# Differential attention: GpSimd scales and adds the two exponentials from the thirteenth step on

## The chip, the cores and the metric

One core of one Trainium2 chip. The time is device microseconds of one execution; three runs of the kernel before are given. Engines: TensorE (PE in the profile, its weight loads PEld), VectorE (DVE), ScalarE (ACT), GpSimd (POOL), SyncE (SP).

## What is computed

The program is two residual blocks of a model of width 1024 on 1024 rows, all in float32: an mLSTM and pooling mixer, a windowed attention, then a block with gated linear attention beside differential attention, a convolutional feed-forward part and a gated embedding. The change lies in the differential attention of the second block. Cut to what matters:

```python
for blk in range(T // Q_BLOCK):                       # 8 blocks of 128 queries
    q0 = blk * Q_BLOCK
    k_end = q0 + Q_BLOCK
    s = jnp.einsum('bqhmd,bkhmd->bhmqk', q[:, q0:k_end], k[:, :k_end])   # 4 heads, m = 0, 1
    s = jnp.where(mask, s, -1e30)
    pr = jax.nn.softmax(s, axis=-1)
    w = pr[:, :, 0] - lam * pr[:, :, 1]
    outs.append(jnp.einsum('bhqk,bkhd->bqhd', w, v[:, :k_end]))
o = rms_norm(jnp.concatenate(outs, axis=1), norm_g) * (1.0 - lam_init)
```

So for each block and head there are two softmaxes over the same keys, and the second is subtracted from the first with a factor before the product with the values.

## The kernel before

The parts of the second block are written as five instruction streams, one for each engine, that meet at semaphores; nothing reorders them. `diff_part` is one of these parts. Its work is 32 steps j = 4 bi + h (query block bi, head h), of width kw = 128 n columns, n = bi + 1 key chunks. What a step does, with the line in the profile:

- TensorE, `scores` (L3359): the products of queries and keys for m = 0 and 1 into the PSUM tile S. For j from 2 to 15 S holds two steps side by side (`s_at`), so that scores(j) wait for the maxima of step j-2; from step 16 it holds one, and scores(j) wait for both maxima of step j-1.
- VectorE, `biggest` (L3475), twice: reads S and the tile `chunk_mask`, writes the scaled, masked scores into `pb` (in the room of HT, so the profile calls it HT) and their maximum into `neg_max`. `pb` has four places, by j % 4.
- ScalarE, `probs` (L3417), twice: the exponential in place in `pb`, and its sum into `sums`.
- VectorE, `weights` (L3482, L3483, L3485): the reciprocal of the sums; the factor `second_share` (cw), one number for each row; and the combination, second exponential times factor plus first, into the first half of `pb`. Division by the first sum is left to the end of a block.
- TensorE, `turn` (L3369): n transposes of the combined tile into TP. ScalarE, `take` (L3425): TP to SBUF. TensorE, `pv` (L3378): the product with the values into O.
- Once a block: ScalarE's `norm` (L3431 and the root behind it), VectorE's `out` (L3491, L3493), TensorE's `turn_diff` (L3318), ScalarE's `diff_hi` (L3442) and VectorE's `diff_lo` (L3506), which split the result into a rounded high part and a low part for the next product.

The order on TensorE in loop index j is scores(j), turn(j-2), pv(j-3), on VectorE biggest(j, 0), biggest(j, 1), weights(j-1), on ScalarE probs(j, 0), take(j-2), probs(j, 1). In the loop indices 16 to 23 VectorE also does an eighth of a weight split each (L412). GpSimd's stream in this part loads the vectors for lambda, fills the mask (L3338, L3340) and loads a norm vector; the next thing in its queue is the load of rows for the output projection (L526), which waits for the last `diff_lo`.

Of the kernel before, what the change touches and what calls it, by code (L numbers as in the profile page):

```python
# [29 lines left out]
ALU = mybir.AluOpType  # L30
# [6 lines left out]
P = 128  # L37
# [3232 lines left out]
def diff_part(K, st, mix):  # L3270
# [7 lines left out]
    nc, i = K.nc, K.i  # L3278
    lam_init = 0.8 - 0.6 * math.exp(-0.3 * 0)
    NJ = 4 * XT  # L3280
    gla_steps = [1, 3, 5, 7, 9, 11, 13, 15]
    K.ZLr = [nc.alloc_sbuf_tensor_at("z_lo_gla", [P, XT, 4, P], F32R, offset=K.offset["Zg"]),
             nc.alloc_sbuf_tensor_at("z_lo_diff", [P, 4, T], F32R, offset=K.offset["dQT"])]
# [3 lines left out]
    pb = room[:, 0:8 * T].rearrange("p (j m n) -> p j m n", m=2, n=T)  # L3287
    wt = room[:, 8 * T:10 * T].rearrange("p (j n) -> p j n", n=T)
    nm = K.sb(st, "neg_max", [P, NJ, 2])
    sm = K.sb(st, "sums", [P, NJ, 2])  # L3290
    rc = K.sb(st, "recip_sums", [P, NJ, 2])
    cw = K.sb(st, "second_share", [P, NJ])
    lam = K.sb(st, "lam", [P, 4])
# [11 lines left out]
    s_in, s_nm, s_p, s_msk = K.sem("df_in"), K.sem("df_max"), K.sem("df_probs"), K.sem("df_mask")  # L3305
    s_s = [K.sem(f"df_scores{m}") for m in range(2)]
    s_w, s_t, s_tr, s_pv = K.sem("df_weights"), K.sem("df_turned"), K.sem("df_turned_read"), K.sem("df_pv")
    s_lam, s_le, s_rs, s_z = K.sem("df_lam_arg"), K.sem("df_lam_exp"), K.sem("df_rs"), K.sem("df_z")
    s_gt, s_gh, s_gl = K.sem("df_gla_turned"), K.sem("df_gla_hi"), K.sem("df_gla_lo")
    s_zt, s_zh, s_zl = K.sem("df_z_turned"), K.sem("df_z_hi"), K.sem("df_z_lo")  # L3310
# [19 lines left out]
    def s_at(j):  # L3330
        return 512 * ((j + 1) % 2) if 2 <= j < 16 else 0

    def gpsimd(g):
        mix.sines(g)
        for n, name in enumerate(("lam_q1_2", "lam_k1_2", "lam_q2_2", "lam_k2_2")):
            g.dma_start(lv[:, n, :], i[name].to_broadcast([P, 64])).then_inc(s_in, 16)
        mix.done(g)
        g.memset(msk[:, :], 0.0).then_inc(s_msk, 1)  # L3338
        g.wait_ge(s_msk, 1)
        g.memset(msk[0:64, T - 64:T], NEG).then_inc(s_msk, 1)  # L3340
        g.wait_ge(s_in, 64)
        g.dma_start(gn[:, :], i["diff_norm_2"].to_broadcast([P, 512])).then_inc(s_in, 16)

    def tensor(pe):
        def scores(j):
# [43 lines left out]

        for j in range(NJ + 6):  # L3390
            if j == 18:
                pe.wait_ge(s_gl, XT)
            if j < NJ and j % 4 == 0:
                mix.ready(pe, j // 4 + 1)
# [70 lines left out]
    def vector(v):  # L3465
        ch = Chain(v, K.v_chain, K.vn)
        mix.left(v)
        v.wait_ge(s_msk, 2)

        def biggest(j, m):  # L3470
            kw = (j // 4 + 1) * P
            v.wait_ge(s_s[m], j + 1)
            if j >= 4:
                v.wait_ge(s_t, j - 3)
            v.tensor_tensor_reduce(pb[:, j % 4, m, 0:kw], S[:, m, s_at(j):s_at(j) + kw], msk[:, T - kw:T], -0.125, -NEG,  # L3475
                                   ALU.add, ALU.min, nm[:, j, m:m + 1]).then_inc(s_nm, 1)

        def weights(j):

            kw = (j // 4 + 1) * P  # L3480
            v.wait_ge(s_p, 2 * j + 2)
            ch.link(v.reciprocal(rc[:, j, :], sm[:, j, :]))  # L3482
            ch.link(v.scalar_tensor_tensor(out=cw[:, j:j + 1], in0=sm[:, j, 0:1], scalar=lam[:, 3:4], in1=rc[:, j, 1:2],  # L3483
                                           op0=ALU.mult, op1=ALU.mult))
            v.scalar_tensor_tensor(out=pb[:, j % 4, 0, 0:kw], in0=pb[:, j % 4, 1, 0:kw], scalar=cw[:, j:j + 1],  # L3485
                                   in1=pb[:, j % 4, 0, 0:kw], op0=ALU.mult, op1=ALU.add).then_inc(s_w, 1)

        def out(bi):
            v.wait_ge(s_rs, bi + 1)
            r = ss[:, 1, bi, :]  # L3490
            ch.link(v.tensor_tensor(r, r, rc[:, 4 * bi:4 * bi + 4, 0], ALU.mult))  # L3491
            for h in range(4):
                ins = v.scalar_tensor_tensor(out=K.QT[:, h, bi * P:(bi + 1) * P], in0=O[:, bi % 2, h * P:(h + 1) * P],  # L3493
                                             scalar=ss[:, 1, bi, h:h + 1], in1=gn[:, h * P:(h + 1) * P],
                                             op0=ALU.mult, op1=ALU.mult)
            ins.then_inc(s_z, 1)

        def gla_lo(r):
            v.wait_ge(s_gh, r + 1)
            v.tensor_tensor(ZL[:, r, :, :], TP[:, 512:1024].rearrange("p (k t) -> p k t", t=P),  # L3500
                            K.ZH[:, 0:4, r * P:(r + 1) * P].bitcast(F32), ALU.subtract).then_inc(s_gl, 1)

        def diff_lo(bi):
            v.wait_ge(s_zh, bi + 1)
            at = slice(bi * P, (bi + 1) * P)
            v.tensor_tensor(ZLD[:, :, at], O[:, bi % 2, :].rearrange("p (k t) -> p k t", t=P),  # L3506
                            K.ZH[:, 4:8, at].bitcast(F32), ALU.subtract).then_inc(s_zl, 1)

        for j in range(NJ + 6):
            if 16 <= j < 24:  # L3510
                K.split_lo(v, ("out2", 0, 1), j - 16, 8)
            if j < NJ:
                biggest(j, 0)
                biggest(j, 1)
            if j == 0:
                v.wait_ge(s_in, 64)
                for n in range(2):
                    v.wait_ge(s_lam, n)
                    v.tensor_tensor_reduce(lp[:, :], lv[:, 2 * n, :], lv[:, 2 * n + 1, :], 1.0, 0.0, ALU.mult, ALU.add,
                                           lam[:, n:n + 1]).then_inc(s_lam, 1)  # L3520
            if j == 6:
                v.wait_ge(s_in, 80)
                ch(v.tensor_scalar(gn[:, :], gn[:, :], 1.0 - lam_init, None, ALU.mult))
            if j == 1:
                v.wait_ge(s_le, 1)

                ch.link(v.tensor_tensor(lam[:, 2:3], lam[:, 1:2], lam[:, 0:1], ALU.subtract))
                ch.link(v.tensor_scalar(lam[:, 3:4], lam[:, 2:3], -lam_init, None, ALU.add))
            if 1 <= j <= NJ:
                weights(j - 1)  # L3530
            if j - 1 in gla_steps:
                gla_lo((j - 1) // 2)
            if j >= 8 and j % 4 == 0:
                out((j - 8) // 4)
            if j >= 10 and j % 4 == 2:
                diff_lo((j - 10) // 4)
        diff_lo(XT - 1)
        K.vn = ch.n

    return Part(sync, gpsimd, tensor, scalar, vector, turn_diff, (XT - 1,), None, done, taken, done)  # L3540


# [470 lines left out]
def phase_gla_in(K):  # L4013
# [7 lines left out]
    with ExitStack() as st:  # L4021
        diff = diff_part(K, st, mix)
# [94 lines left out]
```

## Time and profile before

| | us |
|---|---|
| median of 3 runs | 3333.32 (3331.22 to 3338.41) |
| span of the profiled execution | 3330.9 |
| TensorE busy in it | 3262.9 (98%) |
| VectorE, ScalarE, GpSimd busy | 1781.2, 1524.0, 113.7 |

The page gives a span for the profiled execution and no other time; the span runs from the first to the last instruction. The stage of the change lies from about 2235 us (first scores) to 2357 us (first product of the output projection). Idle time of an engine counts where TensorE waits for it.

### The profile page before, as it was taken

Reading aid. Unit: us, or ns where it says so; the run is one execution under the profiler, and the core shown is the slowest. Engines: PE = TensorE matmul, PEld = TensorE weight load, DVE = VectorE, ACT = ScalarE, POOL = GpSimd, SP = SyncE. Lnnn points to the kernel's source line nnn. Section 1 sums busy time; section 2 is a strip of 40 time slices with the busy share of each in tenths; the row PEclk is TensorE's granted clock in tenths of the full one; section 3 lists DMA queues with packets and bytes.
Section 4 is the critical chain, followed back from the end, with each engine's and each line's share of the span. In section 5 each row is a group of like instructions: output and inputs, shape, how many; then the busy total and the mean of one; then the engine's idle time right before and its main releaser. Section 6 shows DMA issues by size and latency. Waiting matters only on the chain. (4 is left out here: it accounts for less than half of the span.)

```text
span 3330.9 us, 42983 instructions
## 1 busy us (share of the span) xinstructions
PE 3262.9 (98%) x17616; PEld 2669.0 (80%) x17616; DVE 1781.2 (53%) x2768; ACT 1524.0 (46%) x2424; POOL 113.7 (3%) x245
## 2 busy tenths in 40 slices
PE   7999999999999999999999999998999999999998
PEld 5988888898888787887887877776778888878886
DVE  7554444544445567532886634358556445444555
ACT  5343434434334345125786534228435444443456
POOL 2000000000000000001000000000000000000000
PEclk9999999999999999999999999999999999999999
DMA  5202011111443567022301711110332111134464
GB/s 208 72 1 83 29 60 52 55 58 41 143 137 107 218 218 254 26 54 84 78 2 42 209 42 51 31 51 1 133 115 57 46 43 51 51 113 155 175 215 145
DMA packets 186819, 308.39 MB, mean 93 GB/s; under 512 B 28011, under 2 KB 122064, under 8 KB 186496
## 3 DMA queue, kind: packets, MB, share of 16 engines
q1 hardware_dynamic: 164432, 226.68, 21.2%
q0 software_dynamic: 21120, 78.90, 6.9%
q8 instruction: 140, 2.29, 0.3%
q14 instruction: 55, 0.45, 0.0%
q10 hardware_dynamic: 1072, 0.07, 0.0%
HBM read 269.87 MB, written 35.75 MB: 92 GB/s over the span
## 5 line engine op out<-in xcount | busy, mean ns | idle before, releaser
L412 DVE TENSOR_TENSOR W_rounded<-W,W_rounded 128x2048 fp32r<-128x2048 f32 (+2 forms) x184 | 350.7, 1906 | 439.5 <-ACT W_rounded L403 436.1
L403 ACT ACTIVATE W_rounded<-W 128x2048 fp32r<-128x2048 f32 (+1 forms) x172 | 292.9, 1703 | 400.3 <-DMA W<-in_w_down 113.8
L3656 PE MATMUL G<-HT_rounded,W_rounded 128*128 128x512 f32 x1584 | 453.4, 394 | 1.0 <-DVE W_rounded L3593 1.0
L3656 PEld LDWEIGHTS G<-HT_rounded,W_rounded 128*128 128x128 f32 x1584 | 298.5, 188 | 69.8 <-DVE W_rounded L3593 1.3
L2592 PE MATMUL G<-W_rounded,r_y_rounded 128*128 128x512 f32 x960 | 227.7, 397 | 1.0 <-DVE W_rounded L412 0.8
L2592 PE MATMUL G<-W_rounded,x_hi 128*128 128x512 f32 x704 | 220.7, 395 | 3.7 <-DVE W_rounded L412 2.7
L2592 PEld LDWEIGHTS G<-W_rounded,r_y_rounded 128*128 128x128 f32 x960 | 179.8, 188 | 45.4 <-DVE W_rounded L412 1.4
L1153 PE MATMUL G<-W_rounded,HT_rounded 128*128 128x512 f32 x640 | 213.7, 415 | 0.0
L3656 PE MATMUL G<-HT_lo_ffn,W_rounded 128*128 128x512 f32 x528 | 208.8, 395 | 0.0
L2218 PE MATMUL G<-HT_rounded,W_rounded 128*128 128x512 f32 (+1 forms) x768 | 207.8, 355 | 0.0
L1197 PE MATMUL G<-HT_rounded,W_rounded 128*128 128x512 f32 (+1 forms) x768 | 206.6, 355 | 1.0 <-PEq L652 1.0
L2936 PE MATMUL G<-W_rounded,HT_rounded 128*128 128x512 f32 x640 | 203.1, 399 | 0.0
L2592 PEld LDWEIGHTS G<-W_rounded,x_hi 128*128 128x128 f32 x704 | 132.4, 189 | 34.0 <-DVE W_rounded L412 4.6
L2218 PEld LDWEIGHTS G<-HT_rounded,W_rounded 128*128 128x128 f32 x768 | 136.5, 188 | 24.8 <-issue 3.5
L1197 PEld LDWEIGHTS G<-HT_rounded,W_rounded 128*128 128x128 f32 x768 | 135.8, 188 | 22.4 <-issue 1.2
L2936 PEld LDWEIGHTS G<-W_rounded,HT_rounded 128*128 128x128 f32 x640 | 118.4, 188 | 28.2 <-issue 2.0
L1153 PEld LDWEIGHTS G<-W_rounded,HT_rounded 128*128 128x128 f32 x640 | 120.1, 188 | 25.1
L2592 PE MATMUL G<-W_rounded,act_turned_rounded 128*128 128x512 f32 x352 | 139.6, 397 | 0.0
L1197 PE MATMUL G<-HT_lo,W_rounded 128*128 128x512 f32 (+1 forms) x384 | 136.4, 355 | 0.0
L2218 PE MATMUL G<-HT_lo,W_rounded 128*128 128x512 f32 (+1 forms) x384 | 136.4, 355 | 0.0
L1388 DVE SCALAR_TENSOR_TENSOR c_state<-c_state,decay_all,CC 128x514 f32<-128x514 f32 x64 | 48.0, 750 | 156.7 <-PE CC L1182 156.7
L1654 PE MATMUL G<-W_rounded,HT_rounded 128*128 128x512 f32 x416 | 131.5, 397 | 0.0
(501 smaller groups left out, 6598.1 us busy)
## 6 DMA issues: line engine op xcount, KB each, us to landing
W<-in_w_down SPq DMA_DIRECT2D x33, 1024.0 KB, 4.9
W<-in_ab_w_out SPq DMA_DIRECT2D x32, 1024.0 KB, 5.7
W<-in_w_up SPq DMA_DIRECT2D x44, 512.0 KB, 5.1
W<-in_ab_w_in SPq DMA_DIRECT2D x20, 1024.0 KB, 8.8
W<-in_w_mod SPq DMA_DIRECT2D x8, 2048.0 KB, 8.3
x_rows<-r_xt POOLq DMA_DIRECT2D x32, 512.0 KB, 5.3
W<-in_c_w_out SPq DMA_DIRECT2D x24, 512.0 KB, 6.9
r_xt<-x_rows POOLq DMA_DIRECT2D x24, 512.0 KB, 5.0
```

The costliest lines, as they stand in the source:

```text
L403: ins = a.activation(self.half(key, True)[:, at], self.half(key, False, False)[:, at], ACT.Copy)
L412: ins = v.tensor_tensor(self.half(key, False)[:, at], self.half(key, False, False)[:, at], self.half(key, True)[:, at].bitcast(F32), ALU.s ...
L1153: ins = pe.matmul(G[:, K.par(key), :], x[y][:, 4 * kh + k, r * P:(r + 1) * P], wv[z][:, k, :], start=(kh == 0 and k == 0 and (y, z) == SPL ...
L1197: ins = pe.matmul(G[:, K.par(key), 0:n], wv[y][:, k, cc], x[z][:, k, c0:c0 + n], start=(k == 0 and (y, z) == SPLIT_PASSES[0]), stop=(k == ...
L1388: v.scalar_tensor_tensor(out=cs[:, d, :, :], in0=cs[:, d, :, :], scalar=dec[:, d, h, c:c + 1], in1=prod, op0=ALU.mult, op1=ALU.add).then_i ...
L1654: ins = pe.matmul(bank(key), x[y][:, 4 * kh + k, r * P:(r + 1) * P], w[z][:, k, :], start=(kh == 0 and k == 0 and (y, z) == SPLIT_PASSES[0 ...
L2218: ins = pe.matmul(bank(key, n), w[y][:, k, cc], x[z][:, k, c0:c0 + n], start=(k == 0 and (y, z) == SPLIT_PASSES[0]), stop=(k == KT - 1 and ...
L2592: ins = pe.matmul(slot(r)[:, n * 512:(n + 1) * 512], x[y], w[z][:, k, n * 512:(n + 1) * 512], start=(kk == 0 and k == 0 and (y, z) == SPLI ...
L2936: ins = pe.matmul(bank(key), x[y][:, 4 * kh + k, r * P:(r + 1) * P], w[z][:, k, :], start=first, stop=last)
L3656: ins = pe.matmul(bank(("up", j, half))[:, rc * 512:rc * 512 + 512], w[a][:, k, c], x[b][:, 2 * rc:2 * rc + 2, :], start=(k == 0 and a == ...
```

## The change

From step 12 on (`GPS_FROM`) VectorE computes the reciprocal and the factor only and signals a new semaphore. GpSimd waits for it, multiplies the second exponential in place by the factor, waits for its own result, and adds it to the first, then signals `s_w`, for which the turn waits. Steps 0 to 11 are as before.

```diff
+    GPS_FROM = 12
...
+    s_cw, s_c2 = K.sem("df_share"), K.sem("df_second_scaled")
...
+        for j in range(GPS_FROM, NJ):
+            g.wait_ge(s_cw, j - GPS_FROM + 1)
+            kw = (j // 4 + 1) * P
+            g.tensor_scalar(pb[:, j % 4, 1, 0:kw], pb[:, j % 4, 1, 0:kw], cw[:, j:j + 1], None, ALU.mult).then_inc(s_c2, 1)
+            g.wait_ge(s_c2, j - GPS_FROM + 1)
+            g.tensor_tensor(pb[:, j % 4, 0, 0:kw], pb[:, j % 4, 0, 0:kw], pb[:, j % 4, 1, 0:kw], ALU.add).then_inc(s_w, 1)
...
-            ch.link(v.scalar_tensor_tensor(out=cw[:, j:j + 1], in0=sm[:, j, 0:1], scalar=lam[:, 3:4], in1=rc[:, j, 1:2],
-                                           op0=ALU.mult, op1=ALU.mult))
-            v.scalar_tensor_tensor(out=pb[:, j % 4, 0, 0:kw], in0=pb[:, j % 4, 1, 0:kw], scalar=cw[:, j:j + 1],
-                                   in1=pb[:, j % 4, 0, 0:kw], op0=ALU.mult, op1=ALU.add).then_inc(s_w, 1)
+            cw_of = v.scalar_tensor_tensor(out=cw[:, j:j + 1], in0=sm[:, j, 0:1], scalar=lam[:, 3:4], in1=rc[:, j, 1:2],
+                                           op0=ALU.mult, op1=ALU.mult)
+            if j < GPS_FROM:
+                ch.link(cw_of)
+                v.scalar_tensor_tensor(out=pb[:, j % 4, 0, 0:kw], in0=pb[:, j % 4, 1, 0:kw], scalar=cw[:, j:j + 1],
+                                       in1=pb[:, j % 4, 0, 0:kw], op0=ALU.mult, op1=ALU.add).then_inc(s_w, 1)
+            else:
+                cw_of.then_inc(s_cw, 1)
```

VectorE's instructions around the end of the seventh block, before (the maxima are the lines called ISA):

```order
L3482 RECIPROCAL recip_sums<-sums 128x2
L3483 SCALAR_TENSOR_TENSOR second_share<-sums,lam,recip_sums 128x1
L3485 SCALAR_TENSOR_TENSOR HT<-HT,second_share 128x896
L3475 ISA HT,neg_max<-S,chunk_mask 128x1024
L3475 ISA neg_max 128x1
```

and in the changed kernel, whose lines lie 8 to 12 further down:

```order
L3490 RECIPROCAL recip_sums<-sums 128x2
L3491 SCALAR_TENSOR_TENSOR second_share<-sums,lam,recip_sums 128x1
L3483 ISA HT,neg_max<-S,chunk_mask 128x1024
L3483 ISA neg_max 128x1
L3483 ISA HT,neg_max<-S,chunk_mask 128x1024
```

The combination is gone; the maxima of the next step follow the factor directly. GpSimd's queue in the same part of the changed kernel, from the mask on:

```order
L3340 MEMSET chunk_mask 128x1024
L3342 MEMSET chunk_mask 64x64
L3344 DMA diff_norm_all<-in_diff_norm 128x512
L3348 ISA
L3348 TENSOR_SCALAR HT<-HT,second_share 128x512
L3350 TENSOR_TENSOR HT<-HT 128x512
```

Forty instructions (a TENSOR_SCALAR and a TENSOR_TENSOR for each of steps 12 to 31) and one ISA stand now between the norm vector's load and the loads of L526.

## Rows read from the trace of the kernel before

**Rows 1.** The page, part 1: busy time, share of the span, instructions
```profile
PE 3262.9 (98%) x17616; PEld 2669.0 (80%) x17616; DVE 1781.2 (53%) x2768; ACT 1524.0 (46%) x2424; POOL 113.7 (3%) x245
```

**Rows 2.** Windows: start:end, length, busy PE, PEld, DVE, ACT, POOL, PEclk, DMA share, GB/s
```profile
2265.70:2281.10 15.40, 12.80 (x71) 8.50 (x70) 12.19 (x39) 11.95 (x38) 0.00 (x0) 0.89 0.00 1
2281.10:2295.70 14.60, 12.39 (x90) 9.24 (x90) 14.24 (x40) 11.99 (x34) 0.00 (x0) 1.00 0.01 1
2295.70:2311.40 15.70, 14.43 (x102) 10.46 (x102) 15.26 (x39) 12.79 (x33) 0.00 (x0) 1.00 0.01 2
2311.40:2328.10 16.70, 16.44 (x112) 11.70 (x112) 15.50 (x34) 13.97 (x32) 0.00 (x0) 1.00 0.00 1
```

**Rows 3.** Waits from 2281 to 2357 us: total, times, longest (us)
```profile
PEld TP L3369 <- DVE HT L3485: 8.8, 13, 1.5
...
PEld S L3359 <- DVE neg_max L3475: 2.4, 8, 0.5
...
PE S L3359 <- DVE neg_max L3475: 1.6, 5, 0.5
```

**Rows 4.** Timeline, TensorE: start us, us, engine, line, op, [idle before <-releaser]
```profile
2319.94 1.77 PE L3359 MATMUL S<-dKT,dQT 64*128 64x512 f32 x8
...
2337.60 1.99 PE L3359 MATMUL S<-dKT,dQT 64*128 64x512 f32 x8
...
2342.10 1.99 PE L3359 MATMUL S<-dKT,dQT 64*128 64x512 f32 x8
...
2348.23 1.09 PE L3369 MATMUL TP<-ident,HT 128*128 128x128 f32 x8 [1.34 <-DVE HT L3485]
...
2352.14 1.06 PE L3369 MATMUL TP<-ident,HT 128*128 128x128 f32 x8 [1.03 <-ACT HT L3425]
...
2354.83 0.60 PE L3318 MATMUL O<-ident,dQT 128*128 128x128 f32 x4
```

**Rows 5.** Timeline, VectorE, the same stretch
```profile
2321.74 1.09 DVE L3475 CUSTOM_DVE_ANT_0 HT<-S,chunk_mask 128x896 f32<-128x896 f32 x1 [0.34 <-PE S L3359]
...
2339.61 1.23 DVE L3475 CUSTOM_DVE_ANT_0 HT<-S,chunk_mask 128x1024 f32<-128x1024 f32 x1 [0.42 <-PE S L3359]
...
2341.91 0.16 DVE L3482 RECIPROCAL recip_sums<-sums 128x2 f32<-128x2 f32 x1
2342.10 0.22 DVE L3483 SCALAR_TENSOR_TENSOR second_share<-sums,lam,recip_sums 128x1 f32<-128x1 f32 x1
...
2346.89 1.28 DVE L3485 SCALAR_TENSOR_TENSOR HT<-HT,second_share 128x1024 f32<-128x1024 f32 x1
```

**Rows 6.** Groups of VectorE by form: busy us, mean ns | idle before
```profile
L3475 DVE CUSTOM_DVE_ANT_0 HT<-S,chunk_mask 128x1024 f32<-128x1024 f32 x8 | 9.5, 1219 | 1.0 <-PE S L3359 1.0
...
L3475 DVE CUSTOM_DVE_ANT_0 HT<-S,chunk_mask 128x512 f32<-128x512 f32 x8 | 5.2, 686 | 2.8 <-PE S L3359 2.8
L3485 DVE SCALAR_TENSOR_TENSOR HT<-HT,second_share 128x1024 f32<-128x1024 f32 x4 | 5.1, 1285 | 0.1
...
L3485 DVE SCALAR_TENSOR_TENSOR HT<-HT,second_share 128x512 f32<-128x512 f32 x4 | 3.0, 752 | 0.1
```

**Rows 7.** GpSimd: two lines (durations ns, first and last start), timeline
```profile
L3338 POOL MEMSET chunk_mask<- x1: 959/959/959, 2150.7 to 2150.7; 128x1024 f32 x1
...
L3340 POOL MEMSET chunk_mask<- x1: 172/172/172, 2151.8 to 2151.8; 64x64 f32 x1
...
2363.48 1.59 POOL L526 DMA_DIRECT2D r_xt<-x_rows  x3 [210.95 <-DVE z_lo_diff L3506]
```

**Rows 8.** Windows of six us in the same stage, columns as in Rows 2
```profile
2240.00:2246.00 6.00, 5.22 (x21) 3.49 (x23) 4.13 (x23) 3.64 (x16) 0.00 (x0) 0.58 0.00 0
2252.00:2258.00 6.00, 3.74 (x26) 2.37 (x25) 5.21 (x21) 5.84 (x24) 0.00 (x0) 1.00 0.01 3
2258.00:2264.00 6.00, 5.66 (x28) 3.43 (x26) 3.65 (x13) 4.72 (x15) 0.00 (x0) 0.72 0.00 0
...
2282.00:2288.00 6.00, 4.59 (x38) 3.62 (x35) 5.85 (x19) 5.19 (x18) 0.00 (x0) 1.00 0.00 0
```

## The prediction

> **What bounds the kernel now.** I read the page first: TensorE is busy 98% of the span, VectorE 53%, GpSimd 3% [rows 1]. So time is made where TensorE stands still or runs slowly, and the question is which waits of TensorE the edit touches. It touches one stage, differential attention, which runs from about 2235 to 2357 us, and of it the steps 12 to 31. I cut them at the starts of the scores of steps 12, 16, 20, 24 and 28 [rows 2], so that a stretch is one query block of four heads, n = 4 to 8 key chunks wide. A step lasts 15.4/4 = 3.85 us at n = 4, 3.65 at 5, 3.93 at 6 and 4.18 at 7; at n = 8 the scores of steps 28 to 31 lie (2342.10 - 2328.1)/3 = 4.67 apart [rows 2, 4]. TensorE and VectorE share the bound: VectorE is busy 14.24 of 14.60 and 15.26 of 15.70 us at n = 5 and 6, TensorE 16.44 of 16.70 at n = 7. From 2281 to 2357 us TensorE waits 8.8 us for the operation that the change takes from VectorE, and 2.4 + 1.6 us for VectorE's maxima [rows 3]. This is what a faster VectorE could give back.
>
> **The loop that sets a step.** TensorE's order is scores(j+1), turn(j-1), pv(j-2), scores(j+2). turn(j-1) waits for weights(j-1), which VectorE does only after the maxima of step j, which wait for scores(j). From n = 5 there is one score buffer, so scores(j+1) wait for the maxima of j too. In this ring two steps pass from scores(j) to scores(j+2). At n = 8 its parts are [rows 4, 5]:
> - scores start to first maximum, 2337.60 to 2339.61: 2.01 us (1.80 at n = 7, 2319.94 to 2321.74, so 0.21 for each chunk);
> - two maxima, 2339.61 to 2341.91: 2.30 us (one takes 1219 ns at 1024 columns and 686 at 512 [rows 6], so 0.27 less for a pair with each chunk less);
> - reciprocal and share, 2341.91 to 2342.32: 0.41 us;
> - combination, now 1.285 us on VectorE [rows 6];
> - turn and pv at full width, the last turn's start to the next turn of another kind, 2352.14 to 2354.83: 2.69 us, 0.34 for a chunk.
> Today this ring is not the tight one, since combining ends while TensorE is still in the scores: 2.01 + 2.30 + 0.41 + 1.29 + 0.06 + 2.69 = 8.76 us for two steps, 4.38 for one, below the 4.67 that other work makes of it. The 0.06 us is a release: the combination that began at 2346.89 ended at 2348.17, and its turn began at 2348.23 [rows 4, 5].
>
> **Removed.** Twenty combinations on VectorE, four each at five widths, 0.75 to 1.285 us. Alone this is 4 x (0.75 + 0.88 + 1.02 + 1.15 + 1.29) = 20 us of VectorE's time (ends from [rows 6], the widths between by the slope). Its cover is TensorE and the ring, so it is worth at most the 4.0 us in which TensorE waits for maxima. In the forecast the ring takes all of that again: I count zero.
>
> **Added.** GpSimd gets a scale and an add for each of twenty steps, in series with the ring, and two more releases. No row shows GpSimd computing on wide tiles. The nearest are its memsets: 0.959 us for 1024 columns and 0.172 for 64 [rows 7], so 0.82 ns for a column of one stream and 0.12 us for an instruction. A scale reads one stream and writes one, an add reads two and writes one. The lower end is one memset's pass for each operation (2 passes, streams side by side), the upper end is one pass for each stream (2 + 3 = 5). I take 4: one for the scale, three for the add, because a memset is the simplest thing the engine does, and an operation with two inputs is farthest from it, while a scale is nearest. So the pair costs G(n) = 0.24 + 4 x 0.82 x 0.128 n = 0.24 + 0.42 n: 3.60 us at n = 8, 2.34 at n = 5, against 1.29 and 0.88 on VectorE.
> GPSIMD Engine Reference, section 3.1 (the Trainium skill), puts a two-input add there at about 2.6 cycles an element, 4497 ns for 2048 columns, and calls one-input work roughly line-rate. An estimate from that page is 2.3 us for the add at 1024 and G near 3.3 us, and the sum below would be about 2 us smaller. No row here shows it.
>
> **The sum.** Two steps at n = 8 now take 2.01 + 2.30 + 0.41 + 3 x 0.06 + 3.60 + 2.69 = 11.19 us, one step 5.60. Each chunk less takes 0.21 + 0.27 + 0.42 + 0.34 = 1.24 off two steps:
>
> | n | step after | step before | steps | more |
> |---|---|---|---|---|
> | 8 | 5.60 | 4.67 | 3 | 2.8 |
> | 7 | 4.98 | 4.18 | 4 | 3.2 |
> | 6 | 4.36 | 3.93 | 4 | 1.7 |
> | 5 | 3.74 | 3.65 | 4 | 0.4 |
> | 4 | 3.12 | 3.85 | 4 | 0 |
>
> At n = 4 other waits hold the step; they cover G. This is 8.1 us. **The tail:** after the last scores nothing lies beside G. Counted from their start at 2342.10, the maxima are done at +4.31, the share at +4.72, G(30) at +8.5, G(31) behind it on GpSimd at +12.0 us. Today the last turn is at 2352.14, +10.0 [rows 4]: 2.0 us more. **The clock:** TensorE's granted clock was 0.72 (between 2.4 and 1.2 GHz) in the six us after a stretch with 3.74 of 6 us busy, and stayed 1.00 where 4.59 of 6 were busy [rows 8]. The steps at n = 7 and 8 keep it busy some 80%, above both, but ahead of turn(30) it would stand for about 3 us. I count one fall, 0.28 x 6 = 1.7 us, and between none and several for the range.
> Waits behind the change: GpSimd's queue holds nothing but the input loads of the next part, which waited 211 us up to 2363.48 [rows 7] for the last low half of the attention output, so they lose nothing beyond the stage's own delay. The extra instruction ahead of the first scale (ISA in the order) can go out once the mask is filled at 2150.7 us, some 120 us before the first scale: nothing. ScalarE's copies follow the turns and have slack in a longer step.
> Sum: 8.1 + 2.0 + 1.7 = 11.8 us on the profiled span of 3330.9, or 3342.7. The median of the runs, 3333.3, lies 2.4 above that span, and I add it: **3345.1 us**. One pass more or less moves G by 0.105 n us and half of it goes into each step: 5.0 us over the steps and up to 1.7 in the tail. Five passes give 3352; three give about 3338.
>
> **Rivals.** What this kernel's measurement can tell from no change is about 0.2%, 6.7 us.
> (A) *GpSimd is quick, no slower than before.* With two passes G is 1.9 us at n = 8, two steps take 9.51 us, and the steps gain or lose a tenth of a microsecond; the tail is again set by the copy ahead of the last turn. Then VectorE's relief stands against it: +0.6 us in steps of n = 7 and 8, up to -4.0 for the maxima. Time 3330 to 3337. It decides at some 3.1 passes, where the sum falls under 6.7 us. For it: GpSimd fills a column in 0.82 ns, faster than VectorE's 1.04 ns for a column (1285 less 752 ns over 512 [rows 6]) of the combination. Against it: that is for writing alone.
> (B) *GpSimd's reads and VectorE's maxima exclude each other.* The maxima read the mask from SBUF beside the scores. If they can't run during a scale or an add, the pair and the maxima are one chain: at n = 8, 2.30 + 0.41 + 0.18 + 3.60 = 6.49 us a step, then 5.80, 5.11, 4.42 and, at n = 4, under the old 3.85. More than before: 3 x 1.82 + 4 x (1.62 + 1.18 + 0.77) = 19.7, with tail and clock 23.4, or 3356.7. The profile has no wide GpSimd work beside VectorE, so nothing excludes it.
> SBUF — State Buffer (the Trainium skill), section Who interferes with whom, says a VectorE instruction with two SBUF inputs contends with a GpSimd instruction that reads SBUF, and one with a single SBUF input doesn't. The maxima have one in PSUM. By that page only the small share operation and the weight split would be held, and (B) would not happen; no run shows it yet.
> (C) *The clock falls again and again.* From 2240 to 2264 us, with waits in most steps, two of four stretches of six us had 0.58 and 0.72 [rows 8]. If the new waits do the same for the 60 us of n = 6 to 8, five falls of 1.7 make +8.5 beyond the sum less the one counted: 3352.
> (D) *Faster by more than 0.2%.* Beyond A's -4.0 us it would need the clock, or ScalarE's waits before the turns, to gain another 3 us; no row promises it. Time 3325.
>
> **How the numbers follow.** The forecast (3 to 5 passes, ring bound) has 0.60, A 0.20, B 0.11, C 0.06, D 0.03. Slower by over 0.2%: 0.60 + 0.11 + 0.06 = 0.77; within it 0.20; faster 0.03. The range reaches down into A, to 3335, and up to B's time, to 3358.
>
> **What would show it.** GpSimd's scale at 1024 columns near 1.0 us and its add near 2.6. Steps of about 5.6 us at n = 8 and 5.0 at n = 7, no change at n = 4. TensorE waiting for GpSimd's add at the turns, some 1 us a step, in place of VectorE's combination; waits for maxima near zero. VectorE's busy time 20 us less. A turn that waits for no GpSimd row, or maxima with gaps while their scores are done, would make the ring wrong (A, B). A clock under 1.0 before 2345 us would speak for C. The prediction is wrong if steps don't grow with n.

## The result and the profile after

The median of four runs is 3366.95 us (3365.66 to 3370.56), against 3334.22 us before (four runs, 3331.22 to 3338.41): 32.7 us more between the medians. The recorded ratio is 1.0092 with an interval of 1.008 to 1.0104, that is some 31 us (27 to 35). Forecast was 3345.1, with a range that ended at 3358. The direction held, the size did not.

The profiled execution has a span of 3363.9 us, 33.0 more than before. Its marks split this into three: the first scores start at 2240.3 in place of 2234.5 us (5.8), the first product of the output projection at 2389.35 in place of 2356.97 (another 26.6 for the stage), and 0.6 after it. The changed steps are not yet running in the 5.8; the first experiment asks about them.

The windows of the changed kernel, cut at the starts of the scores of steps 12, 16, 20, 24, 28 and 31 (columns as in [rows 2]):

```profile
2270.60:2286.00 15.40, 10.78 (x69) 7.01 (x68) 11.28 (x37) 13.23 (x41) 6.83 (x5) 1.00 0.00 1
2286.00:2304.40 18.40, 13.69 (x89) 9.84 (x88) 12.73 (x35) 11.07 (x31) 11.53 (x8) 0.91 0.00 1
2304.40:2324.40 20.00, 14.36 (x101) 10.35 (x100) 12.21 (x34) 13.58 (x33) 15.59 (x9) 1.00 0.00 1
2324.40:2347.30 22.90, 18.13 (x114) 12.85 (x113) 11.36 (x30) 13.56 (x31) 16.68 (x8) 0.93 0.01 1
2347.30:2368.80 21.50, 15.31 (x93) 11.01 (x92) 10.20 (x25) 13.97 (x28) 18.20 (x8) 0.92 0.00 0
2368.80:2389.30 20.50, 15.16 (x100) 13.56 (x100) 6.00 (x14) 8.34 (x20) 11.75 (x5) 0.83 0.00 1
```

A step now takes 15.4/4 = 3.85 us at n = 4, 4.60 at 5, 5.00 at 6, 5.72 at 7, and 21.5/3 = 7.17 at 8, where before it took 3.85, 3.65, 3.93, 4.18 and 4.67. VectorE, busy 15.26 of 15.70 us at n = 6 before [rows 2], is busy 12.21 of 20.0. The last stretch, from the last scores to the projection, is 20.5 us; it was 14.87.

The waits between 2270 and 2390 us (PE is TensorE's products; PEld is its queue of weight loads, which runs beside them):

```profile
DVE HT L3483 <- PE S L3367: 41.4, 18, 5.4
PEld TP L3377 <- POOL HT L3350: 38.8, 19, 5.5
PE TP L3377 <- POOL HT L3350: 29.0, 16, 5.3
ACT HT L3425 <- DVE neg_max L3483: 28.8, 15, 3.9
```

The 8.8 us for VectorE's combination [rows 3] were waits of the weight queue, most of them while the products of the scores were still running. The products themselves waited for it once, 1.3 us, ahead of turn(30). In the kernel before, from 2281 to 2357 us:

```profile
PE TP L3369 <- DVE HT L3485: 1.3, 1, 1.3
```

Like compared with like, TensorE's products now wait 29.0 us for GpSimd's add in place of 1.3, and its weight queue 38.8 in place of 8.8. The waits of TensorE for maxima, 2.4 us in the weight queue and 1.6 in the products before, are gone; it is VectorE now that waits, 41.4 us, for scores. GpSimd's two operations by width:

```profile
L3348 POOL TENSOR_SCALAR HT<-HT,second_share 128x1024 f32<-128x1024 f32 x4 | 11.4, 2843 | 6.1 <-DVE second_share L3491 6.0
...
L3350 POOL TENSOR_TENSOR HT<-HT 128x1024 f32<-128x1024 f32 x4 | 9.4, 2350 | 0.3
...
L3348 POOL TENSOR_SCALAR HT<-HT,second_share 128x512 f32<-128x512 f32 x4 | 6.4, 1590 | 122.2 <-DVE second_share L3491 122.2
...
L3350 POOL TENSOR_TENSOR HT<-HT 128x512 f32<-128x512 f32 x4 | 5.1, 1264 | 0.3
```

The add takes 2.35 us at 1024 columns, near the 2.6 of the forecast. The scale, with one wide input, takes 2.84, where the forecast had 1.0. TensorE's steps at full width (starts of scores at 2354.68, 2359.91 and 2368.81, turns behind them):

```profile
2354.68 1.99 PE L3367 MATMUL S<-dKT,dQT 64*128 64x512 f32 x8
...
2359.91 1.99 PE L3367 MATMUL S<-dKT,dQT 64*128 64x512 f32 x8
2364.84 1.97 PE L3377 MATMUL TP<-ident,HT 128*128 128x128 f32 x8 [2.94 <-POOL HT L3350]
...
2368.81 1.99 PE L3367 MATMUL S<-dKT,dQT 64*128 64x512 f32 x8
...
2378.96 1.97 PE L3377 MATMUL TP<-ident,HT 128*128 128x128 f32 x8 [5.34 <-POOL HT L3350]
...
2384.22 1.37 PE L3377 MATMUL TP<-ident,HT 128*128 128x128 f32 x8
...
2389.35 0.72 PE L2592 MATMUL G<-W_rounded,z_hi 128*128 128x512 f32 x2
```

Two things are to be seen. The turns at 2364.84 and 2378.96 start within 0.1 us of the end of an add of GpSimd (2362.44 + 2.35 and 2376.56 + 2.34), after 2.94 and 5.34 us without work. And both last 1.97 us in place of 1.09: the granted clock was 0.50 from 2364.84 to 2366.81 and from 2378.96 to 2384.20 us.

### The profile page after: what moved, and what is told of

It reads as the page before. It is cut to its first block and busy times, and to the rows that moved or that the text cites. A ratio compares the mean times of both kernels' runs of the same rounds, so it can differ in the third digit from the quotient of the medians.

```text
span 3363.9 us, 43005 instructions
## 1 busy us (share of the span) xinstructions
PE 3268.6 (97%) x17616; PEld 2672.6 (79%) x17616; DVE 1766.0 (52%) x2748; ACT 1524.6 (45%) x2424; POOL 193.8 (6%) x285
## 3 DMA queue, kind: packets, MB, share of 16 engines
q1 hardware_dynamic: 164432, 226.68, 20.9%
```

## Experiments

All were compared with the kernel before on the same chip. "Steps" are distances between starts of scores, as above; the kernel before has 3.84, 3.65, 3.92, 4.19 and 4.65 us for n = 4 to 8 and a tail of 14.87.

| run | ratio to before | n=4 | 5 | 6 | 7 | 8 | tail |
|---|---|---|---|---|---|---|---|
| changed kernel | 1.0092 (1.0080 to 1.0104) | 3.85 | 4.61 | 5.00 | 5.72 | 7.17 | 20.5 |
| 1 no step moved | 0.9998 (0.9988 to 1.0007) | 3.84 | 3.65 | 3.92 | 4.20 | 4.65 | 14.9 |
| 2 add only | 1.0004 (0.9995 to 1.0013) | 3.84 | 3.65 | 4.14 | 4.43 | 4.79 | 14.8 |
| 3 constant factor | 1.0082 (1.0067 to 1.0097) | 4.23 | 4.62 | 5.66 | 6.02 | 6.16 | 21.1 |
| 4 last block alone | 1.0032 (1.0019 to 1.0044) | 3.84 | 3.65 | 3.92 | 4.20 | 6.47 | 20.3 |
| 5 scale as a product | 1.0042 (1.0027 to 1.0057) | 4.11 | 3.98 | 4.63 | 5.25 | 5.66 | 18.5 |
| 6 turns one later | 1.0023 (1.0012 to 1.0033) | 3.70 | 3.81 | 3.93 | 4.26 | 4.76 | 22.8 |
| 7 every second step | 1.0090 (1.0075 to 1.0105) | 3.80 | 4.95 | 5.26 | 5.51 | 7.79 | 20.9 |
| 8 second step, turns later | 1.0021 (1.0012 to 1.0030) | 3.97 | 3.83 | 4.18 | 4.45 | 4.74 | 20.8 |
| 9 turns later, VectorE alone | 1.0012 (1.0003 to 1.0020) | 3.97 | 3.65 | 3.92 | 4.19 | 4.64 | 17.6 |
| 10 product, turns later | 1.0004 (0.9996 to 1.0013) | 3.71 | 3.54 | 4.09 | 4.12 | 4.57 | 18.0 |
| 11 weight split on GpSimd | 0.9995 (0.9987 to 1.0003) | 3.84 | 3.52 | 3.76 | 4.22 | 4.65 | 14.9 |

**Run 1: no step moved.**

```diff
-    GPS_FROM = 12
+    GPS_FROM = 32
```

> The changed kernel with its first GpSimd step set to 32, so that no step is moved and only the two unused semaphores stay. Theory R (the ring of two steps through GpSimd makes the loss): time as before within 0.2%, the stage from first scores to first product of the output projection 122.5 us as before, and also the 5.8 us by which the first scores came later in the changed kernel's profile are gone or vary from run to run. Rival P (the program as such is slower, by its semaphores or by where its code lies): 3 to 6 us of the loss stay.

The time is that of before, and the profiled execution of this run has its first scores at 2239.9 us with no step moved. In the profiles of all the runs this start lies between 2234.5 and 2243.3. So P falls: the 5.8 us ahead of the stage are the spread from one execution to the next, and the profile of before was an early one. What the change costs is in the stage.

**Run 2: the add alone.**

```diff
-            g.tensor_scalar(pb[:, j % 4, 1, 0:kw], pb[:, j % 4, 1, 0:kw], cw[:, j:j + 1], None, ALU.mult).then_inc(s_c2, 1)
-            g.wait_ge(s_c2, j - GPS_FROM + 1)
```

> The scale on GpSimd is left out and the exponentials are added unscaled (the weights are not the reference's). R: GpSimd's part of the ring falls from 5.3 to 2.4 us at n = 8, so two steps take 2.01 + 2.30 + 0.41 + 0.12 + 2.35 + 2.69 = 9.88 us, a step 4.9 against 4.67 before and 7.2 in the changed kernel; the loss falls from 33 to 1 to 6 us. Rival Q (any use of GpSimd beside VectorE holds VectorE up, whatever its length): about half of the loss stays, 12 to 16 us.

Q falls, and the ring holds in numbers: 4.9 us for a step at n = 8 was worked out, 4.79 measured; at n = 7 the same sum gives (1.80 + 2.03 + 0.41 + 0.12 + 2.09 + 2.35)/2 = 4.40, and 4.43 was measured. Twenty adds of up to 2.36 us on GpSimd, longer than the combination of 1.285 us that they replace, cost the kernel nothing that its time can tell (0.0004, interval -1.7 to +4.3 us). In the steps the profile shows 2.3 us, 0.14 to 0.24 for each at n = 6 to 8. TensorE's waits for the adds are there, but short (in the products 6.6 us, in the weight queue 15.9):

```profile
PEld TP L3375 <- POOL HT L3348: 15.9, 17, 1.8
```

The ring speaks of pairs of steps, so pairs test it best: it gives 9.88 us at n = 8, and from scores 28 to 30 and 29 to 31 there are 9.87 and 9.91. At n = 6 it is not what binds: it would give 3.85 us a step, and 4.14 was measured. Part of that is VectorE, held by an add (more on this below, at rival B): a small product of a block's norms took 1.50 us in place of 0.16, the maxima behind it came late, and the scores at 2308.00 waited for them.

```profile
2303.20 1.50 DVE L3501 TENSOR_TENSOR o_ss<-o_ss,recip_sums 128x4 f32<-128x4 f32 x1
...
2308.00 0.70 PE L3365 MATMUL S<-dKT,dQT 64*128 64x512 f32 x2 [0.90 <-DVE neg_max L3481]
```

**Run 3: a constant in place of the row factor.**

```diff
-            g.tensor_scalar(pb[:, j % 4, 1, 0:kw], pb[:, j % 4, 1, 0:kw], cw[:, j:j + 1], None, ALU.mult).then_inc(s_c2, 1)
+            g.tensor_scalar(pb[:, j % 4, 1, 0:kw], pb[:, j % 4, 1, 0:kw], 0.5, None, ALU.mult).then_inc(s_c2, 1)
```

> GpSimd's scale takes the constant 0.5 in place of the factor of each row (the weights are not the reference's). If the row factor, read as a pointer, makes the scale dear: it falls from 2.84 us at 1024 columns to 1.0 to 1.3, and the loss falls by 60 x 0.05 = about 12 to 15 us. If a scale costs that much by itself: 2.8 us again and the time of the changed kernel.

```profile
L3348 POOL TENSOR_SCALAR HT<-HT 128x1024 f32<-128x1024 f32 x4 | 11.1, 2769 | 4.4 <-DVE second_share L3491 4.1
```

2.77 us against 2.84: the factor's place is worth 0.07 us. The operation with a scalar is dear on GpSimd whatever the scalar is. The time stays near that of the changed kernel. (Its steps at n = 6 and 7 are longer and at n = 8 shorter than there; the granted clock fell in other places, to 0.72, 0.73 and 0.72 in windows of six us from 2310, 2322 and 2334 us.)

**Run 4: the last block alone.**

```diff
-    GPS_FROM = 12
+    GPS_FROM = 28
```

> Only steps 28 to 31 go to GpSimd. R: three steps at n = 8 grow by 1.75 to 2.5 us each and the tail by 3.7 to 5.7: 9 to 13 us over before. Rival Q': the loss grows with the number of moved steps alone (4 of 20): 5 to 6.5 us.

Over before 10.7 us by the ratio, inside R's 9 to 13; the interval, 6.3 to 14.7 us, just touches Q' with 5 to 6.5. The profile decides between them: three steps longer by 1.8 us each and a tail longer by 5.4 make 10.9. A fifth of the moved steps carries a third of the loss: the widest steps have the longest G, and the tail (20.3 against 14.9) is paid whole.

**Run 5: the scale written as a product of two tensors.**

```diff
-            g.tensor_scalar(pb[:, j % 4, 1, 0:kw], pb[:, j % 4, 1, 0:kw], cw[:, j:j + 1], None, ALU.mult).then_inc(s_c2, 1)
+            g.tensor_tensor(pb[:, j % 4, 1, 0:kw], pb[:, j % 4, 1, 0:kw], cw[:, j:j + 1].to_broadcast([P, kw]), ALU.mult).then_inc(s_c2, 1)
```

> GpSimd's scale is written as a product of two tensors, the second the row factor spread over the columns, in place of an operation with a scalar. If a scalar operation on GpSimd is dear by its kind: the product costs what the add costs, 2.35 us at 1024 columns, GpSimd's pair 4.8 in place of 5.3, half of the 0.5 us less in each step at n = 8, and the loss falls by 3 to 5 us. If each operation on GpSimd that reads a factor beside a wide tile costs 2.8 us: no change.

```profile
L3350 POOL TENSOR_TENSOR HT<-HT 128x1024 f32<-128x1024 f32 x4 | 9.4, 2346 | 0.3
...
L3348 POOL TENSOR_TENSOR HT<-HT,second_share 128x1024 f32<-128x1024 f32 x4 | 7.6, 1894 | 4.6 <-DVE second_share L3491 4.5
```

The same result for 1.89 us in place of 2.84, even less than the add. The loss fell by more than half, 30.7 to 14 us, and by much more than the 3 to 5 us expected. That expectation was too small on both counts: G fell by 0.95 us and not by 0.5, and the clock's part was left out of it. With G = 1.89 + 2.35 the ring gives (2.01 + 2.30 + 0.41 + 0.18 + 4.24 + 2.69)/2 = 5.9 us at n = 8, 5.66 measured, and 5.3 at n = 7, 5.25 measured. In pairs it gives 11.83 us at n = 8, and 11.62 and 11.77 were measured. The changed kernel's 7.17 lay 0.8 above its ring. The turns of run 5 waited 0.2 to 1.9 us for adds between 2282 and 2364 us, and the clock stayed at 1.00 there.

**Run 6: the turns one loop index later.**

```diff
-            if 2 <= j < NJ + 2:
-                turn(j - 2)
+            if 3 <= j < NJ + 3:
+                turn(j - 3)
...
-            if 3 <= j < NJ + 3:
-                pv(j - 3)
+            if 4 <= j < NJ + 4:
+                pv(j - 4)
...
-            if 2 <= j < NJ + 2:
-                take(j - 2)
+            if 3 <= j < NJ + 3:
+                take(j - 3)
```

> As the changed kernel, but TensorE turns step j-3 and multiplies step j-4 in loop index j, one later than now, and ScalarE copies one later; GpSimd's work then lies in a ring of three steps. R: the ring gives 12.86/3 = 4.3 us at n = 8 and no longer binds; GpSimd's own 5.4 us a step does at n = 8, 4.8 at n = 7, 4.2 at n = 6: 3 x 0.7 + 4 x 0.6 + 4 x 0.3 = 6 us, and the tail 5.7 + up to 3: the loss falls from 33 to 10 to 16 us. If it is not the ring but contention or the clock: 25 us or more stay.

With all forty operations still on GpSimd at the same durations, the loss falls from 0.92% to 0.23%. The steps are within 0.16 us of before at every width. Only the order on TensorE and ScalarE was changed, so the loss was the ring's (with what the clock added to it: most of the waits went too, and every window of six us from 2282 to 2360 us has a clock of 1.00). That is less than the 10 to 16 us I expected. GpSimd's own throughput, which I expected to bind at 5.4 us a step, did not show in these distances (4.76 at n = 8) but in the tail, 22.8 us. GpSimd waited for a factor only 3 times (15 in the changed kernel), so it ran almost without a pause and fell behind the scores:

```profile
POOL HT L3348 <- DVE second_share L3491: 123.2, 3, 119.1
...
PEld TP L3377 <- POOL HT L3350: 11.9, 10, 2.8
```

(The first row's longest wait, 119.1 us, is the one before the first scale.) TensorE's weight queue still waits 11.9 us for adds and its products 6.2, against 38.8 and 29.0 in the changed kernel.

**Run 7: every second step.** Each engine signals its own semaphore, and the turn waits for the one of its step.

```diff
-    GPS_FROM = 12
+    GPS_STEPS = list(range(12, 31, 2))
...
-            pe.wait_ge(s_w, j + 1)
+            on_g = sum(s <= j for s in GPS_STEPS)
+            pe.wait_ge(*((s_wg, on_g) if j in GPS_STEPS else (s_w, j + 1 - on_g)))
...
-            if j < GPS_FROM:
+            if j not in GPS_STEPS:
```

> Only the even ones of steps 12 to 31 go to GpSimd, the odd ones stay on VectorE (the turn waits for a semaphore of each engine). R: the ring spans two steps, and every second one goes through GpSimd, so each pair of steps still takes 12.86 us at n = 8: most of the loss stays, 20 to 27 us. Rival N (the loss goes with the number of moved steps): half, 14 to 17 us.

Half of the work moved, the whole loss: 1.0090 against 1.0092, some 30 us (25 to 35), where R had 20 to 27. N is out. TensorE's last steps show why:

```profile
2355.34 2.01 PE L3367 MATMUL S<-dKT,dQT 64*128 64x512 f32 x8
...
2360.20 1.99 PE L3367 MATMUL S<-dKT,dQT 64*128 64x512 f32 x8
2365.54 1.89 PE L3378 MATMUL TP<-ident,HT 128*128 128x128 f32 x8 [3.35 <-POOL HT L3350]
...
2369.76 1.99 PE L3367 MATMUL S<-dKT,dQT 64*128 64x512 f32 x8
2371.68 1.09 PE L3378 MATMUL TP<-ident,HT 128*128 128x128 f32 x8
...
2380.35 1.97 PE L3378 MATMUL TP<-ident,HT 128*128 128x128 f32 x8 [5.79 <-POOL HT L3350]
```

The turns of even steps wait 3.35 and 5.79 us for GpSimd's add, those of odd steps for nothing; but the scores of the next step stand behind the turn that waits, so a pair of steps takes about what it took when both waited. It is even longer at n = 5 (9.9 us against 9.2) and above the ring at n = 8 (pairs of 13.8 and 14.4 us for 12.86). At least in part that is the clock: every window of six us from 2270 to 2312 us had 0.72 to 0.93, and four windows from 2348 to 2384 had 0.61 to 0.88.

**Run 8: every second step, and the turns later.** The edits of runs 6 and 7 together.

> Even steps on GpSimd and turns one loop index later. R: ring of three steps 4.3 us and GpSimd 5.4 us for two steps, both below the 4.67 us of today at n = 8: the time of the kernel before plus up to 3 us of a longer tail; VectorE's relief of 10 us gives back at most the 4.0 us of waits for maxima: 3 us less to 3 us more than before. If GpSimd's work disturbs VectorE's: over 7 us more.

0.21% over before, 7 us (4 to 10), where 3 at most were expected; over 7 was to be the sign that GpSimd's work disturbs VectorE's, so the time alone excludes neither. The steps at n = 8 are back at 4.74, and those of n = 5 to 7 lie 0.2 to 0.3 above, 2.8 us in all. There VectorE was disturbed: six of its factors between 2291 and 2336 us ended with an add and took 3.0 us more together than usual, and the products of the scores waited 6.0 us for maxima up to 2340 us, against 1.6 before and 3.1 in run 9. One case of it:

```profile
2308.07 1.06 DVE L3492 SCALAR_TENSOR_TENSOR second_share<-sums,lam,recip_sums 128x1 f32<-128x1 f32 x1
...
2313.01 1.45 PE L3367 MATMUL S<-dKT,dQT 64*128 64x512 f32 x6 [1.52 <-DVE neg_max L3484]
```

The tail is 20.8 us:

```profile
2351.66 1.06 PE L3378 MATMUL TP<-ident,HT 128*128 128x128 f32 x8 [2.05 <-ACT HT L3434]
2352.56 1.95 PE L3387 MATMUL O<-dV,HT 128*128 128x128 f32 x16
2356.67 1.41 PE L3378 MATMUL TP<-ident,HT 128*128 128x128 f32 x8 [2.16 <-POOL HT L3350]
2357.87 3.31 PE L3387 MATMUL O<-dV,HT 128*128 128x128 f32 x16
```

Two of the last three turns wait, 2.05 us for ScalarE and 2.16 for GpSimd, and behind the second of them the products run near half the clock (3.31 us for sixteen in place of 1.95).

**Run 9: the turns later, VectorE alone.** The edit of run 6 with `GPS_FROM = 32`.

> All steps on VectorE as in the kernel before, turns one loop index later. It tells how much of the 0.2% of the two runs with later turns is the longer tail and not GpSimd. R: steps as before, the tail 14.9 + 2 to 3 us: 1 to 4 us over before. If the later turn itself is the loss in those two runs: 7 us over before.

0.12%, some 4 us; the tail is 2.7 us longer, the steps are as before. So of the 0.23% and 0.21% of runs 6 and 8 about half is the later turn itself, by the middle values; the intervals are wide beside them. And it settles something on the kernel before: the combination that a turn needs is now a whole loop index old, no product of TensorE waits for it any more, and no step is shorter. The row for the weight queue is still there all the same, 7.3 us in place of 8.8, so it never measured a loss:

```profile
PEld TP L3377 <- DVE HT L3495: 7.3, 12, 0.9
```

**Run 10: the product form and the turns later.**

> The product form of the scale and turns one loop index later, all of steps 12 to 31 on GpSimd. GpSimd's pair is 4.24 us at n = 8, below the 4.67 us of a step, so neither the ring of three steps (2.01 + 2.30 + 0.41 + 0.18 + 4.24 + 2.69 = 11.83, 3.9 us a step) nor GpSimd binds: steps as before, the tail 14.9 + 3 to 6 us: 2 to 6 us over before, less than with the dearer scale (0.23%). If VectorE's relief of 20 us were worth anything once the ring is off: steps below 3.65, 3.92, 4.20 and 4.65 us.

1.0004, no difference from before that can be told. This is the change's own aim with its two costs taken out: VectorE does twenty combinations less, the ring has three steps (TensorE's products wait 0.3 us for an add, in the tail), and the steps are 0.07 to 0.13 us shorter at n = 4, 5, 7 and 8 and 0.17 longer at 6, in all 4 x (-0.13 - 0.11 + 0.17 - 0.07) - 3 x 0.08 = -0.8 us. The tail is 3.1 us longer.

**Run 11: other work on GpSimd.** The kernel before, with the eight weight subtractions of steps 16 to 23 on GpSimd; VectorE waits once, at j = 24, for their end.

```diff
-            if 16 <= j < 24:
-                K.split_lo(v, ("out2", 0, 1), j - 16, 8)
+            if j == 24:
+                v.wait_ge(K.w_lo, K.pl.halves[("out2", 0, 1)] + 1)
...
+        for n in range(8):
+            g.wait_ge(s_w, 14 + n)
+            K.split_lo(g, ("out2", 0, 1), n, 8)
```

> The kernel before, with other work moved: GpSimd takes the eight weight subtractions of steps 16 to 23 (128x256 each, on no ring) from VectorE. By the ring's logic work with nobody waiting for it costs nothing on GpSimd; VectorE is relieved of 8 x 0.33 = 2.6 us in the steps where it is busiest (n = 5 and 6): 0 to 2.6 us less than before. If GpSimd's two-input subtractions hold VectorE's two-input operations as the adds did: up to 8 x 0.6 = 5 us more.

```profile
2288.64 0.73 POOL L412 TENSOR_TENSOR W_rounded<-W,W_rounded 128x256 fp32r<-128x256 f32 x1 [2.80 <-DVE HT L3488]
2291.72 0.73 POOL L412 TENSOR_TENSOR W_rounded<-W,W_rounded 128x256 fp32r<-128x256 f32 x1 [2.35 <-DVE HT L3488]
```

Eight operations of 0.73 us (two are shown) for which nobody waits. The steps at n = 5 and 6 fell from 3.65 to 3.52 and from 3.92 to 3.76 us, 1.2 us for the eight; the whole kernel is at 0.9995 (0.9987 to 1.0003), which doesn't exclude no change. It is the only version whose steps were shorter at both widths, and it isn't shown to beat the kernel before.

## Why the prediction was wrong

**The step that failed.** The ring held. The term of the sum that was badly off is "I take 4: one for the scale, three for the add": G at n = 8 was put at 3.60 us and measured 5.19, and more than all of the difference is the scale (1.0 us in the forecast, 2.84 measured; the add came out at 2.35 for 2.6). With measured durations, G at n = 8 is 2.84 + 2.35 = 5.19 us, 4.60 at n = 7, 4.04 at 6, 3.47 at 5 and 2.85 at 4. Put into the same sum:

| n | ring with measured G | measured | forecast | before |
|---|---|---|---|---|
| 8 | 12.78/2 = 6.39 | 7.17 | 5.60 | 4.67 |
| 7 | 11.37/2 = 5.69 | 5.72 | 4.98 | 4.18 |
| 6 | 9.99/2 = 5.00 | 5.00 | 4.36 | 3.93 |
| 5 | 8.60/2 = 4.30 | 4.61 | 3.74 | 3.65 |
| 4 | 7.17/2 = 3.59 | 3.85 | 3.12 | 3.85 |

At n = 4 it stays below what other waits make, and nothing changed there, as forecast. The steps sum to 3 x 1.72 + 4 x (1.51 + 1.07 + 0.65) = 18.1 us, in place of 8.1. The tail by the same arithmetic has G(30) done at +10.0 and G(31) at +15.2 us; the last turn started at +15.41 (2368.81 to 2384.22), so 5.4 us in place of 2.0. Together 23.5 us. With nothing but the measured G put in, the forecast would have been 13.4 us higher, 3358.5, just beyond the end of its range.

The medians lie 21.9 us above the forecast. Of this the stage has 15.7: 10.0 in the steps, 3.4 in the tail, and 2.3 by which the rest (4.0, below) was more than the 1.7 counted for the clock. Nearly all that is left are the 5.8 us ahead of the stage, which are spread: the forecast was built on the profile of before with the earliest first scores.

**The clock** was forecast with one fall, 1.7 us, and it fell more than once (C, in part). Between the starts of step 12's scores and of the projection the stage grew by 27.5 us (118.73 against 91.24), so 4.0 us are left beside the ring and the tail: 1.2 at n = 5, 2.3 at n = 8, 0.3 in the tail and 0.1 at n = 7. The rows show what they are.

```profile
2291.17 1.41 DVE L412 TENSOR_TENSOR W_rounded<-W,W_rounded 128x256 fp32r<-128x256 f32 x1
...
2299.94 2.51 PE L3367 MATMUL S<-dKT,dQT 64*128 64x512 f32 x8
...
2366.60 2.28 PE L3386 MATMUL O<-dV,HT 128*128 128x128 f32 x14
```

- At n = 8 the starts of scores 28 to 31 are 7.38, 5.23 and 8.90 us apart, so pairs are 12.61 and 14.13, for a ring of 12.78. The second pair is 1.35 longer, and turn and products in it (2364.84 to 2368.81) took 3.97 us in place of 2.69: the clock, at 0.50 during the turn. The other 1.0 us has most likely come over from n = 7, since the steps alternate: the last one at n = 7 is a short one (4.89), and the three at n = 8 begin and end with a long one. At n = 7 the products at 2340.07 and the scores at 2342.41 took 2.42 and 2.47 us in place of 1.50 and 1.77, at a granted clock of 0.64 from 2340.07 to 2344.80.
- At n = 5 one part is the clock (the scores at 2299.94 took 2.51 us in place of 1.35, at a granted clock of 0.50). Another is VectorE: the maxima of step 17 began 3.13 us after their scores in place of 1.38, because VectorE stood in a block's norm work and in a weight subtraction that an add held up (1.41 us in place of 0.42).
- In the tail the last turn took 1.37 us in place of 1.06.

How much the clock has in all stays open, since no run holds the waits and takes only the clock away. Averages over a block can't tell it: the window of n = 7 had 0.93, and its steps stayed within 0.03 us of the ring on average.

**The price of the scale.** The upper end of the range for the pair was 5 passes, 4.44 us at n = 8; 5.19 was measured, outside it. The memset was the wrong neighbour for an operation with a scalar: per column it costs (2843 - 1590)/512 = 2.45 ns, three times the memset's 0.82 and more than the add's (2350 - 1264)/512 = 2.12. The reasoning that a scale is "nearest" to a memset, with its fewer streams, put the cheap price on the dear operation. Against the page: from GPSIMD Engine Reference, section 3.1 (the Trainium skill), the prediction had an estimate of 2.3 us for an add of 1024 columns, and 2.35 was measured. The same page of the Trainium skill, in section 4.1 (the prediction has it under 3.1), calls one-input work roughly line-rate, and the one-input scale here was slower than the add. There the measurement decides.

**The rivals.** (A) needed G at some 3.1 passes; run 2 made it true by leaving the scale out, and the loss went, as (A) said. (D) did not happen, and no run was shown to be faster than before. (B) did not happen: the maxima ran beside GpSimd's scale and add at their old durations, as the two engines' timelines show (first scale, then add of step 16):

```profile
2294.50 1.99 POOL L3348 TENSOR_SCALAR HT<-HT,second_share 128x640 f32<-128x640 f32 x1 [2.20 <-DVE second_share L3491]
...
2295.65 0.82 DVE L3483 CUSTOM_DVE_ANT_0 HT<-S,chunk_mask 128x640 f32<-128x640 f32 x1 [0.92 <-PE S L3367]
...
2296.40 0.82 DVE L3483 CUSTOM_DVE_ANT_0 HT<-S,chunk_mask 128x640 f32<-128x640 f32 x1
...
2296.57 1.54 POOL L3350 TENSOR_TENSOR HT<-HT 128x640 f32<-128x640 f32 x1
...
2297.34 0.78 DVE L3491 SCALAR_TENSOR_TENSOR second_share<-sums,lam,recip_sums 128x1 f32<-128x1 f32 x1
```

The two maxima take 0.82 us each, as before. The factor at 2297.34, however, takes 0.78 us in place of 0.22: it ends at 2298.12, and the add at 2298.11. The same happened to the small product of a block's norms in the tail:

```profile
2373.64 2.84 POOL L3348 TENSOR_SCALAR HT<-HT,second_share 128x1024 f32<-128x1024 f32 x1 [3.45 <-DVE second_share L3491]
...
2375.61 0.22 DVE L3491 SCALAR_TENSOR_TENSOR second_share<-sums,lam,recip_sums 128x1 f32<-128x1 f32 x1
...
2376.56 2.34 POOL L3350 TENSOR_TENSOR HT<-HT 128x1024 f32<-128x1024 f32 x1
...
2377.80 1.13 DVE L3503 TENSOR_TENSOR o_ss<-o_ss,recip_sums 128x4 f32<-128x4 f32 x1 [1.96 <-ACT o_ss L484]
```

It took 1.13 us in place of 0.16 and ended with the add (2378.90), while the factor at 2375.61, beside the scale, took its usual 0.22. Five of VectorE's small two-input operations in the stage took longer than usual and ended within 0.03 us of an add, and a weight subtraction that usually takes 0.42 us took 1.41 beside one. So there is an exclusion, and it is the narrow one: SBUF — State Buffer (the Trainium skill), section Who interferes with whom, says that a VectorE instruction with two SBUF inputs contends with a GpSimd instruction that reads SBUF, and the trace agrees for the add. Beside the scale, which reads SBUF too, it agrees in part only: the factor above took its usual 0.22 us, three weight subtractions 0.42, 0.64 and 0.75. There the measurement decides. In the changed kernel it cost little, because VectorE had time to spare, 41.4 us of it; at n = 5, above, and in runs 2 and 8, where VectorE was busier, it reached the scores.

**Removed work.** VectorE's 20 us were counted at zero, and run 10 against run 9 bears this out: with the ring out of the way, taking them off shortens the steps of four widths by 0.07 to 0.26 us and lengthens those of one by 0.17, 1.3 us less in all, and the whole kernel is not shown to be faster. Two readings on the way to that zero were wrong. The 8.8 us were the weight queue's, not time in which TensorE's products stood still (1.3 us). And the 2.4 and 1.6 us for maxima are for the most part the same waits, seen in the weight queue and in the products, so that at most some 1.6 us could have come back, and not 4.0.

**The ISA ahead of the first scale** went out early, as forecast: its instruction in the profile stands at 2158.4 us, 119 us ahead of the first scale.

```profile
L3348 POOLq MODIFY_POOL_CONFIG  x2: 37/37/37, 2158.4 to 2158.4; - x2
```

## What to carry to other kernels

Before work goes to an idle engine, draw the ring that it lies in and count how many steps it spans: the price is the added latency divided by the steps of the ring (half here), for every second step as much as for all, and it vanishes from the steps when the consumer is moved one step on (run 6, which pays for it in the tail) or when nobody waits (run 11). In the profile's waits read the rows of the products; a row of the weight queue can be long while the products run. The busy share of the engine that is relieved tells nothing until it is known that it binds: VectorE was busy 97% of the time in some blocks, and 20 us less on it gained nothing that the time can tell. A scale by a row factor on GpSimd, written as a product of two tensors, took a third less time here than the form with a scalar, and that was worth more than half of the loss.

## What the hardware showed unexpectedly

- On GpSimd, float32 in SBUF, 1024 columns: product with a row factor spread over the columns 1.89 us, add of two wide tiles 2.35, operation with a scalar 2.84 with a row factor and 2.77 with a constant. Why the scalar form is the dearest was not tried further.
- GpSimd's two-input add and VectorE's small two-input operations excluded each other: 0.78 and 1.13 us in place of 0.22 and 0.16, ending within 0.03 us of the add (2.33 us in place of 0.22 in run 10, at 2350.56). In run 8, where VectorE still did every second combination, it went the other way too: an add at 1024 columns took 2.78 us in place of 2.36, begun at 2353.84 while a combination of VectorE's ran.
- After waits of TensorE of 2.94 and 5.34 us the following turns took 1.97 us in place of 1.09, the lower of its two clock levels. After a wait of 2.92 us, at 2352.20 in the same profile, the turn took its usual 0.98 us, at a granted clock of 1.00: the length of the one wait ahead doesn't decide it. In run 5, whose turns waited 0.2 to 1.9 us between 2294 and 2364 us, no six-us window of that stretch has a clock under 1.00.
